# Four stages of a hybrid layer in one block: attention output, merge, output product and feed-forward

## What is computed

```python
branch_a = y.astype(x.dtype) @ w_a            # y: state-space branch, computed before
o = o.transpose(0, 2, 1, 3).reshape(bsz, L, SB_WIDTH)   # attention, computed before
branch_b = o @ w_b
merged = jax.nn.sigmoid(gate_a) * branch_a + jax.nn.sigmoid(gate_b) * branch_b
x = x + merged @ w_out
hf = rmsnorm(x, norm_ffn_g)
x = x + (jax.nn.silu(hf @ w_gate) * (hf @ w_up)) @ w_down
g = jax.nn.sigmoid(rmsnorm(x, norm_ple_g) @ w_ple_gate)
x = x + g * (p.astype(x.dtype) @ w_ple)
```

## Time and profile before

| what | value |
|---|---|
| median of 3 timed runs | 2816.05 us (2813.18 to 2821.95) |
| profiled execution | 2819.61 us |
| its span | 2817.9 us |
| mean granted clock of TensorE | 0.968 |
| TensorE (PE) busy | 2665.3 us, 95% |
| VectorE (DVE) busy | 1518.5 us, 54% |
| ScalarE (ACT) busy | 853.0 us, 30% |
| GpSimd (POOL) busy | 365.1 us, 13% |

### The profile page before, as it was taken

How to read it: one execution, slowest core, us unless ns; L and a number is a source line. 1 busy time by engine, 2 the same in 40 slices (tenths; PEclk the granted TensorE clock), 3 DMA queues, 4 the chain that set the end, 5 groups by cost and what they waited for, 6 DMA issues and landing times. The chain is left out here.

```text
span 2817.9 us, 48052 instructions
## 1 busy us (share of the span) xinstructions
PE 2665.3 (95%) x17088; PEld 2511.3 (89%) x17088; DVE 1518.5 (54%) x2581; ACT 853.0 (30%) x1566; POOL 365.1 (13%) x327
## 2 busy tenths in 40 slices
PE   6999999999987999999979999999999999999798
PEld 6888888887867989999979999899999999999697
DVE  4565655665563766675653343444444444444745
ACT  4443434333332433433341112211111111111533
POOL 0232322322230111111100002100000000000300
PEclk8999999999997999999989999999999999999799
DMA  5444344465432242435345333311111111111012
GB/s 139 95 83 83 98 92 93 88 85 82 90 74 46 32 95 32 96 33 76 51 166 196 138 104 121 131 45 40 43 45 37 45 43 39 45 37 45 29 37 93
DMA packets 331854, 214.31 MB, mean 76 GB/s; under 512 B 117828, under 2 KB 312216, under 8 KB 331672
## 3 DMA queue, kind: packets, MB, share of 16 engines
q1 hardware_dynamic: 331672, 211.98, 32.4%
HBM read 164.51 MB, written 47.41 MB: 75 GB/s over the span
## 5 line engine op out<-in xcount | busy, mean ns | idle before, releaser
L136 ACT ACTIVATE w_hi<-w_raw 128x1024 fp32r<-128x1024 f32 x171 | 180.6, 1057 | 806.8 <-PE f_acc L159 449.4
L159 PE MATMUL f_acc<-operand_hi,w_hi 128*128 128x384 f32 x1056 | 354.1, 335 | 0.0
L159 PE MATMUL f_acc<-operand_lo,w_hi 128*128 128x384 f32 x1056 | 353.5, 335 | 0.0
L159 PE MATMUL f_acc<-operand_hi,w_lo 128*128 128x384 f32 x1056 | 353.5, 335 | 0.0
L1048 POOL TENSOR_TENSOR wgt<-wgt,left 128x128 f32<-128x128 f32 (+2 forms) x224 | 227.5, 1027 | 596.0 <-DVE left L1003 367.0
L674 PE MATMUL acc<-operand_hi,w_hi 128*128 128x384 f32 x792 | 289.3, 365 | 5.5 <-PEq L209 5.5
L143 DVE TENSOR_TENSOR w_lo<-w_raw,w_hi 128x1024 fp32r<-128x1024 f32 x171 | 211.6, 1238 | 151.1 <-ACT w_hi L136 150.0
L159 PE MATMUL sacc<-operand_hi,w_hi 128*128 128x384 f32 x768 | 268.5, 350 | 4.6 <-DVE w_lo L143 3.1
L674 PE MATMUL acc<-operand_hi,w_lo 128*128 128x384 f32 x792 | 268.3, 339 | 0.0
L674 PE MATMUL acc<-operand_lo,w_hi 128*128 128x384 f32 x792 | 267.8, 338 | 0.0
L1003 DVE TENSOR_TENSOR_SCAN left<-keep,left 128x128 f32<-128x128 f32 (+2 forms) x224 | 220.9, 1011 | 74.9 <-ACT keep L898 70.8
(11 more groups left out here) (335 smaller groups left out, 5311.2 us busy)
## 6 DMA issues: line engine op xcount, KB each, us to landing
w_raw<-in_w_in SPq DMA_DIRECT2D x65, 512.0 KB, 9.0
k_cache<-in_cache_k SPq DMA_DIRECT2D x256, 64.0 KB, 2.1
v_cache<-in_cache_v SPq DMA_DIRECT2D x64, 256.0 KB, 5.2
w_raw<-in_w_gate SPq DMA_DIRECT2D x22, 512.0 KB, 3.8
w_raw<-in_w_up SPq DMA_DIRECT2D x22, 512.0 KB, 3.9
w_raw<-in_w_down SPq DMA_DIRECT2D x22, 512.0 KB, 3.7
s_gate_a<-gate SPq DMA_DIRECT2D x24, 192.0 KB, 2.0
s_o<-o_t SPq DMA_DIRECT2D x8, 576.0 KB, 10.4
```

Of the source, the lines that this page charges most:

```text
L136: act.activation(S.w_hi[u0 % 2][:, :], S.raw[u0 % 2][:, :], ACT.Copy).then_inc(S.hi_done, 1)
L159: last = pe.matmul(acc[:, 0:RBN], w[:, k, :], a[:, k, rows], start=(n == 0), stop=(n == 3 * kts - 1 and more is None))
```

## The change

The four stage functions no longer open a block of their own. Each returns its five instruction streams (`Engines`), and `hybrid_step` opens one block in which every engine runs the four streams one behind the other. The three barriers between them are gone; the one ahead of the attention output and the one behind the feed-forward stay. What the barriers kept apart is now ordered by waits on semaphores:

- Eight banks are allocated once; all four stages use the first six, the row sums the last two in turn (`sums`).
- A buffer `spare` of two tiles takes the place of `gate` in the first stage; later its first half holds the x columns of the even output tiles, and its second half the merge's `prod` and then `sq`.
- Merge: TensorE and SyncE wait for the 16 low parts of the first stage (`y_split`).
- Output product: the first pass stands outside the loop, and its first three blocks wait, at their last two k, for the low parts of the merge one by one. The x columns of tile 0 are loaded by `first_x`, between the last store of the first stage and the merge's first loads; those of tile 1 after the merge's last bank was read.
- Feed-forward: the first three blocks wait in the same way for the low parts of the output product. The row sums stand behind block 2 (two of them) and block 3. VectorE makes the low part of the third weight tile ahead of the norm factors, not behind the reads of the first three banks; ScalarE makes its high part ahead of the roots. SyncE waits for the last block of the output product before it loads `x_t`.

The diff without what is only a new indentation:

```diff
-def product_block(S, pe, slot, acc, rhs, rb, ready, free, kts=KT, more=None):
+def product_block(S, pe, slot, acc, rhs, rb, ready, free, kts=KT, more=None, before=None):
...
     for k in range(kts):
+        if before is not None:
+            before(k)
...
+Engines = namedtuple("Engines", "sync tensor scalar vector gpsimd")
...
-def stage_attention_out(nc, S, A, b0, bv0, u0, tiles, next_tiles):
+def stage_attention_out(nc, S, A, ctx, b0, bv0, u0, tiles, next_tiles):
-        gate = [sb(f"gate{n}", [P, ROWS]) for n in range(2)]
+    gate = [S.spare[:, n, :] for n in range(2)]
-        acc = [bank(f"acc{n}") for n in range(6)]
+    acc = S.bank[0:6]
-        S.part_stored = stored
+    S.part_stored, S.y_split = stored, lo_done
-        with nc.Block() as block:
-            @block.sync
-            def _(sp):
+    def sync(sp):
...
+    return Engines(sync, tensor, scalar, vector, None)
...
     # stage_merge
-        prod = [sb(f"prod{n}", [P, RBN]) for n in range(2)]
+    prod = [S.spare[:, 1, rb_cols(n)] for n in range(2)]
+    S.merged = lo_done
...
+        sp.wait_ge(S.y_split, 2 * KT)
         for s in S.part_stored:
             sp.wait_ge(s, DMA_HEAD + 16 * KT // 2)
...
-                pe.wait_ge(S.acc_read_v, HEAD + bv0)
+        pe.wait_ge(S.y_split, 2 * KT)
...
     # stage_out
-        xr = [S.stream[:, n, 0:ROWS].rearrange("p (r c) -> p r c", c=P) for n in range(2)]
+    xr = [v.rearrange("p (r c) -> p r c", c=P) for v in (S.spare[:, 0, :], S.stream[:, 1, 0:ROWS])]
-        sq = [sb(f"sq{n}", [P, RBN]) for n in range(2)]
+    sq = [S.spare[:, 1, rb_cols(2 - n)] for n in range(2)]
-        acc = [bank("acc0"), bank("acc1")]
+    acc = S.bank[0:6]
+    def first_x(sp):
+        sp.wait_ge(S.acc_read_v, HEAD + bv0 - KT * NRB)
+        x_cols(sp, 0, 0)
...
-                x_cols(0, 0)
-                x_cols(0, 1)
+        sp.wait_ge(S.acc_read_v, HEAD + bv0)
+        x_cols(sp, 0, 1)
...
-                with pe.Fori(0, KT // 2) as i:
-                    for n in range(6):
-                        j, rb, a = n // 3, n % 3, acc[n % 2]
+        def block(i, n, before=None):
+            j, rb, a = n // 3, n % 3, acc[n]
...
+        pe.wait_ge(S.merged, 3 * (KT - 2))
+        for n in range(6):
+            def merged_in(k):
+                if n < 3 and k >= KT - 2:
+                    pe.wait_ge(S.merged, 3 * k + n + 1)
+            block(0, n, merged_in)
+        with pe.Fori(1, KT // 2) as i:
+            for n in range(6):
+                block(i, n)
...
     # stage_ffn
-        acc = [bank(f"acc{n}") for n in range(6)]
-        ssum = bank("ssum")
+    acc, sums = S.bank[0:6], S.bank[6:8]
...
+        sp.wait_ge(S.acc_done, HEAD + b0)
         for k in range(KT):
             sp.dma_start(x[:, k, :], S.d_x[k]).then_inc(x_in, 16)
...
-                for rb in range(NRB):
-                    if rb >= 1:
-                        pe.wait_ge(var_done, rb)
-                    pe.matmul(ssum[:, 0:RBN], S.ones[:, :], S.ss[:, rb_cols(rb)], start=True, stop=True)\
+        def sum_up(rb):
+            if rb == 0:
+                pe.wait_ge(S.x_squares, START + 3 * KT)
+            if rb == 2:
+                pe.wait_ge(var_done, 1)
+            pe.matmul(sums[rb % 2][:, 0:RBN], S.ones[:, :], S.ss[:, rb_cols(rb)], start=True, stop=True)\
...
-                pe.wait_ge(S.acc_read_v, HEAD + bv0)
+        pe.wait_ge(S.hf_split, START + 3 * (KT - 2))
         for n in range(6):
-                    up(0, "up0", n)
+            def split_in(k):
+                if n < 3 and k >= KT - 2:
+                    pe.wait_ge(S.hf_split, START + 3 * k + n + 1)
+            up(0, "up0", n, split_in)
+            if n == 2:
+                sum_up(0)
+                sum_up(1)
+            if n == 3:
+                sum_up(2)
...
+        split(u0 + 2, 2, 0, HEAD + b0 + 3)
         for rb in range(NRB):
             act.wait_ge(var_done, rb + 1)
...
-                split(u0 + 2, 2, 0, HEAD + b0 + 3)
         gates(0, "up0")
...
+        split_after(0, "up0", 0)
         for rb in range(NRB):
             dve.wait_ge(sum_done, rb + 1)
...
     # hybrid_step
+            S.bank = [banks.enter_context(nc.psum_tensor(f"bank{n}", [P, 512], F32)) for n in range(8)]
+                S.spare = two.enter_context(nc.sbuf_tensor("spare", [P, 2, ROWS], F32))
+                @block.sync
+                def _(sp):
+                    attention.sync(sp)
+                    S.first_x(sp)
+                    merge.sync(sp)
+                    out.sync(sp)
+                    ffn.sync(sp)
```

955 lines of the change are left out of this document (482 added, 473 removed).

## The result

The changed kernel takes 2794.35 us (median of 4 runs, 2791.55 to 2794.93) where the kernel before took 2819.0 us on the same chip (4 runs, 2813.18 to 2822.96): a ratio of 0.9905, 95% interval 0.989 to 0.992. That is 24.7 us less by the medians, and 24.8 by the two profiled spans (2817.9 and 2793.1). In a second set of runs it was 2796.23 against 2820.9 us, ratio 0.991 (0.9894 to 0.9925). The forecast was 24.1 us less and 2792.0 us.

What follows compares the result with a forecast made beforehand. TensorE, busy 95% of the time, was taken to bound the kernel. Terms 6.4 + 6.9 + 13.2 - 2.0 - 0.45 = 24.1 us less, from a median of 2816.05 to 2792.0 us; range 2788 to 2801.

Steps and rivals of the forecast that it cites:

- What bounds the kernel: Whole kernel: TensorE bounds, busy 2665.3 of 2817.9 us; gaps and half clock at three stage seams cost 26.5 us.
- The seams: Three joints between the four stages: gaps close and clock stays up, gaining 6.4, 6.9 and 13.2 us.
- seam 1: Attention output to merge: a gap of 4.33 us plus low clock of 2.1 us, 6.4 us gained.
- The row sums: Feed-forward start: three row-sum products now stand between blocks, 0.65 us each, 2.0 us given back.
- The norm factors: Feed-forward block 6: norm factors come later, so TensorE waits 0.45 us for bank 0; bounds 0 and 1.5.
- The low part ahead of the factors: Feed-forward third weight tile: low part at 15.0 instead of 29.8, wanted at 27.0; keeps some 3 us.
- SyncE: Before the merge: x columns issued ahead of gate loads fill a DMA hole; 0 to 1 us later, priced 0.
- Late gates: Rival at the merge: store and x columns share DMA engines, gates 5 us later, TensorE waits 3.1; 2797.2 us, chance 0.11.
- Code at the exits of loops: Rival at three loop exits: TensorE enters code not yet run, stalling 2 us each; 2798.0 us, chance 0.10.
- No effect: Rival at the seams: stalls as long as today's gaps, clock falls as now; 2811 us, chance 0.06.
- slower: Rival from 1458 to 2608: without rest the chip grants a low clock; 2832 us at 80 us of it, chance 0.03.
- The sign given for that: Sign of a right forecast: granted clock of 1.00 from the start of the merge to 2600.

Runs made afterwards that it cites:

- The experiment: Changed kernel with VectorE's low part of the third feed-forward weight tile behind the bank reads again and ScalarE's high part behind the roots; ratio 0.9934 to before.

## Why the prediction was right

**What bounds the kernel** held: everything gained lies in the idle time and the low clock of TensorE at three places, and the rest of the kernel kept its distances.

**The seams.** Forecast 6.4, 6.9 and 13.2 us less what comes back. All three gaps are closed: the first gave 4.29 of 4.33 us, and at the other two, where the table has gap and clock in one, the list of waits has no entry left. The only term that was a little small is the low clock behind seam 1. The trace has 15 slow products from 1566.50 on behind a slow first one, and the merge gained 7.97 - 5.40 = 2.6 us beside the gap, not 2.1: the stretch that the 2.1 was read from ends at 1570.60, while the clock is still at 0.50.

**The row sums**: 1790.05 to 1791.52, less the 0.17 of a product, is 1.30 us for two, and 1795.53 to 1796.35 less 0.17 is 0.65 for the third. Forecast 0.65 each.

**The norm factors**: forecast, counted from the seam, the low part at 15.0 and the end of the first bank's read at 27.45, a wait of 0.45. Measured 15.1 (1792.63 - 1777.48) and 27.3 (1804.25 + 0.56 - 1777.48), a wait of 0.26.

**The low part ahead of the factors** was priced at some 3 us for the wait alone. The experiment gave 2.0 more of wait (2.2 in place of 0.3) and 1.5 for the clock that falls behind it, which the prediction had not counted in: 3.5.

**SyncE**: x columns ahead of the gates priced at 0 with 0 to 1 us of delay, margin 2.1 us; measured 0.1 to 1.5 us of delay, scatter included, without effect, and a margin of 1.8 and 1.1.

**The rivals.** Late gates: not here. The store that this rival has land later landed no later: SyncE passed the wait for it 5.3 us behind its issue (1564.62 to 1569.90), before 5.8 (1564.66 to 1570.42). But the chain behind the gates is real, and with four more loads ahead of them it costs 6.9 us. Code at the exits of loops: no stall at any of the three (0.17 us from product to product at the first), and the one stall at an exit that this kernel has is data. No effect, and slower: the clock is 1.00 from the merge on to 2583, so a thousand us with one wait of 0.26 us in them brought no low clock in this kernel. The sign given for that was a clock of 1.00 to 2600; it missed the stall of 3.86 us at 2583, behind which ten products run slow, as they do behind the same stall before the change.

**The level.** The forecast of 2792.0 stands on a median before of 2816.05; with a fourth run it became 2819.0. The gain was forecast as 24.1 and came as 24.7, and the 2.35 us between 2792.0 and 2794.35 are this shift of the base less 0.6.

## What to carry to other kernels

A barrier between two stages costs the bounding engine the tail of every other engine, DMA issues of the sync engine among them, and then a stretch at half clock: here 7 to 8 us each. Price its removal by what the data ask for at each seam, and look at once at the next chain: after the joining, one chain had 1 to 2 us in hand and another was 0.3 us late, and the place of one VectorE instruction (with its ScalarE half) decided over 3.5 us. What is needed only some blocks later (row sums, transposes) should stand behind the first blocks, and what the bounding engine wants first (a weight tile's low part) ahead of long work such as reciprocals.

## What the runs showed of the hardware that I had not expected

**The low clock behind a gap has no fixed price.** Idle times of TensorE, and how many products behind them started 0.32 us apart, the pace at 1.2 GHz, in place of 0.17:

| idle time, us | slow products |
|---|---|
| 1.5 (14 profiles) | none |
| 2.23 | 10 |
| 2.36 | none |
| 2.82 | 17 |
| 2.84 | none |
| 3.14 | none |
| 3.86 (13 profiles, exit of the feed-forward loop) | 8 to 14 |
| 4.16 | 15 |
| 4.97 to 5.23 (4 gaps) | 9, 10, 10 and 16 |
| 5.6 (2 gaps) | 9 and 11 |
| 6.4 and 6.5 | 8 and 8 |
| 7.09 (14 profiles, ahead of the attention output) | 11 to 17 |

Each such product costs 0.15 us, and the first one behind a gap up to 0.3, so a gap costs 0 to 2.8 us on top of itself, and a longer one isn't followed by a longer low stretch. Nor does the place fix it: the gaps of 2.82 and 2.84 us are the same wait in two kernels, with 17 slow products behind one and none behind the other. In eight of the 13 profiles with the stall of 3.86 us the first three to seven products behind it still run at full pace before the clock falls. What decides all this these runs don't show. The Trainium skill, page "TensorE: Matmul & The Clock Gate" (What's actually happening), also has the number of slow products vary from run to run of one kernel. It is also the scatter of the yardstick: the kernel with the x columns behind the gates had 15 and 14 low products, where the changed one had 11 and 10, behind two gaps that both have, which is 1.2 of the 1.3 us by which its yardstick is longer.

**Issuing is not free at a barrier.** The DMA of the sample columns (64 KB) held SyncE for 1.74 us, and as the last instruction ahead of a barrier it lengthened the gap of all engines by 2.3 us together with its neighbour. The neighbour moves 512 KB in rows of the same length and held SyncE for 0.43 us only, so neither the bytes nor the row length alone set this time. What does, these rows don't show.
